# GpSimd takes the adding of squares and every second low half in the gate tiles of a streaming encoder step

## The reference, cut to what matters

```python
xn = rmsnorm(h, norm_mix_g)                  # rsqrt(mean(x*x) + eps), 2048 features
proj = xn @ w_in                             # 2048 x 3584, all in fp32
a = proj[..., :2 * D_CONV]                   # value and gate, 1024 columns each
glu = a[..., :D_CONV] * jax.nn.sigmoid(a[..., D_CONV:])
y = depthwise_conv(glu, 31 taps) + dw_b      # per channel
y = silu(layernorm(y, ln_g, ln_b))
```

## Time and profile before

| | |
|---|---|
| median of 3 runs | 2055.32 us (2044.23, 2055.32, 2055.69) |
| the profiled execution | 2047.77 us, its span 2046.0 us |
| busy in the span | PE 1981.8, DVE 1530.7, ACT 858.1, POOL 718.3 us |
| granted clock of PE, mean | 0.988 |
| slots 1 to 3 of the gate tiles | 32.3 to 51.2 us |
| slots 4 to 15 | 51.2 to 127 us |
| value, key and query | 127 to 220 us |

### The profile page before, as it was taken

One profiled execution on the slowest core, in us unless ns is written; L12 is line 12 of the kernel. 1 busy time (PEld: TensorE's weight loads), 2 busy tenths in 40 slices (PEclk: granted clock), 3 DMA queues, 4 the chain that ended last, 5 costly groups with the idle time before them and its releaser, 6 DMA issues. The chain is left out here.

```text
span 2046.0 us, 29568 instructions
## 1 busy us (share of the span) xinstructions
PE 1981.8 (97%) x11192; PEld 1765.1 (86%) x11192; DVE 1530.7 (75%) x2436; ACT 858.1 (42%) x857; POOL 718.3 (35%) x504
## 2 busy tenths in 40 slices
PE   7999998999899999999999999999999999999997
PEld 6987776998799999999999889988888888888886
DVE  5988745456678788989988987567677777778875
ACT  4340136334334554455454435433434343334343
POOL 2010110220726677587787875011001011114300
PEclk9999998999899999999999999999999999999999
DMA  5464393443344787788888787779998989998983
GB/s 207 164 193 141 116 400 137 153 168 123 127 137 156 247 275 268 272 281 286 274 272 298 265 306 283 294 274 348 340 343 328 343 326 349 364 360 345 372 314 136
DMA packets 101226, 531.27 MB, mean 260 GB/s; under 512 B 19376, under 2 KB 21568, under 8 KB 45792
## 3 DMA queue, kind: packets, MB, share of 16 engines
q1 hardware_dynamic: 71552, 408.93, 55.8%
q0 software_dynamic: 24304, 106.45, 14.4%
q10 hardware_dynamic: 5296, 14.98, 1.9%
HBM read 491.34 MB, written 38.14 MB: 259 GB/s over the span
## 5 line engine op out<-in xcount | busy, mean ns | idle before, releaser
L889 DVE TENSOR_TENSOR wl<-raw,wh 128x2048 fp32r<-128x2048 f32 x310 | 712.4, 2299 | 287.1 <-ACT wh L519 275.5
L519 ACT ACTIVATE wh<-raw 128x2048 fp32r<-128x2048 f32 x310 | 593.3, 1915 | 572.5 <-DMA raw<-in_v 408.4
L1537 PE MATMUL acc<-xhl,wh 128*128 128x448 f32 x2048 | 648.9, 377 | 12.2 <-DVE wl L889 12.2
L1538 PE MATMUL acc<-xhl,wl 128*128 128x224 f32 x2048 | 542.8, 265 | 0.0
L1537 PEld LDWEIGHTS acc<-xhl,wh 128*128 128x128 f32 x2048 | 386.7, 189 | 44.7 <-DVE wl L889 14.6
L1538 PEld LDWEIGHTS acc<-xhl,wl 128*128 128x128 f32 x2048 | 393.2, 192 | 0.0
L2025 POOL DMA_INDIRECT G<-gsum,cell x224 | 348.2, 1554 | 99.7 <-issue 74.8
L1514 PE MATMUL acc<-xhl,wh 128*128 128x288 f32 x768 | 231.7, 302 | 14.8 <-DVE wl L925 14.2
L1515 PE MATMUL acc<-xhl,wh 128*128 128x288 f32 x768 | 228.4, 297 | 0.0
L1516 PE MATMUL acc<-xhl,wl 128*128 128x288 f32 x768 | 227.9, 297 | 0.0
L1514 PEld LDWEIGHTS acc<-xhl,wh 128*128 128x128 f32 x768 | 146.5, 191 | 18.2 <-DVE wl L925 14.2
(11 more groups left out here) (306 smaller groups left out, 2638.8 us busy)
## 6 DMA issues: line engine op xcount, KB each, us to landing
raw<-in_u SPq DMA_DIRECT2D x128, 1024.0 KB
raw<-in_v SPq DMA_DIRECT2D x128, 1024.0 KB
raw<-in_w_mix SPq DMA_DIRECT2D x28, 1024.0 KB
G<-zero SPq DMA_DIRECT2D x16, 1024.0 KB, 13.8
raw<-in_w_out SPq DMA_DIRECT2D x16, 1024.0 KB
raw<-in_w_pq SPq DMA_DIRECT2D x16, 1024.0 KB
gin<-G SPq DMA_DIRECT2D x32, 512.0 KB
h<-hbg ACTq DMA_DIRECT2D x32, 448.0 KB
```

Source lines behind the costliest of these rows:

```text
L519: act.activation(wh[:, n % 4], raw[:, n % 4], ACT.Copy).then_inc(hi_done, 1)
L889: dve.tensor_tensor(wl[:, n % 4], raw[:, n % 4], wh[:, n % 4].bitcast(F32), ALU.subtract).then_inc(lo_done, 1)
L1537: pe.matmul(acc[:, s, 0:2 * NU], wh[:, s, j, :], xu[:, j, 0:2 * NU], start=(j == 0), stop=False)
L1538: ins = pe.matmul(acc[:, s, 0:NU], wl[:, s, j, :], xuh[:, j, :], start=False, stop=(j == DT - 1))
```

## The change

POOL squares two row tiles at a time as before, but adds the results up itself into `sqacc` (in the memory of `gsb`, which is not used yet), without waiting for PE. PE sums `sqacc` by two matmuls, placed between slots 2 and 3. ACT makes the high half of slot 3 before it waits for the sums, DVE the low half of slot 3 before the norm.

In the gate tiles DVE makes only the low halves of even slots from slot 4 on; those of slots 5, 7, 9, 11, 13 and 15 are made by POOL, each behind its multiply of a gate, and counted in the new `odd_lo`. DVE's `lo_done` goes on by two for each even slot.

```diff
@@ ScalarE, glu_iteration @@
-                    if not (last and s >= 4 - AHEAD):
+                    if not (last and s >= 4 - AHEAD) and not (first and s == 1):
                         hi_next(GLU0, i, s)
...
                     if first and s == 0:
+                        hi_next(GLU0, 0, 1)
                         act.wait_ge(eps_ready, 1)
-                        norm_root(0, mis[:, 2], sq_used, 8)
+                        norm_root(0, mis[:, 2], sq_used, 1)
@@ VectorE, glu_iteration @@
-                    if not (last and s >= 4 - AHEAD):
-                        lo_next(GLU0, i, s)
                     if first and s == 0:
+                        lo_next(GLU0, 0, 0)
+                        lo_next(GLU0, 0, 1)
                         norm_recip(0, mis[:, 2])
+                    elif s % 2 == 0 and not (last and s >= 4 - AHEAD):
+                        lo_next(GLU0, i, s, count=2)
@@ TensorE @@
-                pe.wait_ge(lo_done, g + 1)
+                if odd:
+                    pe.wait_ge(odd_lo, 2 * (i - 1) + s // 2 + 1)
+                else:
+                    pe.wait_ge(lo_done, g + 1)
...
             slot(GLU0, 0, 0, xh, xl, before=lambda j: pe.wait_ge(split_lo, j + 1))
-            pe.wait_ge(const_in, 16)
-            squares(0, 2, N)
             for s in range(1, 4):
+                if s == 3:
+                    pe.wait_ge(const_in, 16)
+                    pe.wait_ge(sq_done, 8)
+                    for j in range(2):
+                        ins = pe.matmul(mis[:, 2, 0:N], ones, sqacc[:, j, :], start=(j == 0), stop=(j == 1))
+                    ins.then_inc(sq_used, 1)
                 slot(GLU0, 0, s, xh, xl)
             with pe.Fori(1, 4) as i:
                 for s in range(4):
-                    slot(GLU0, i, s, xh, xl)
+                    slot(GLU0, i, s, xh, xl, odd=s % 2 == 1)
@@ GpSimd @@
-                if n >= 2:
-                    pool.wait_ge(sq_used, n - 1)
                 src = hT[:, 2 * n:2 * n + 2, :]
-                pool.tensor_tensor(sqb[:, n % 2], src, src, ALU.mult).then_inc(sq_done, 1)
+                if n == 0:
+                    pool.tensor_tensor(sqacc[:], src, src, ALU.mult).then_inc(sq_done, 1)
+                    continue
+                pool.wait_ge(sq_done, n)
+                own.done(pool.tensor_tensor(sqb[:, 0], src, src, ALU.mult))
+                own.wait(0)
+                pool.tensor_tensor(sqacc[:], sqacc[:], sqb[:, 0], ALU.add).then_inc(sq_done, 1)
             pool.dma_start(glu[:, :, S0:S0 + HIST], dr["cconv"]).then_inc(hist_in, 16)
...
+            for n in range(8):
+                pool.wait_ge(sig_done, n + 1)
+                pool.wait_ge(acc_free, GLU0 + 4 + 2 * n)
+                if n == 0:
+                    pool.wait_ge(rstd_done, 1)
+                pool.tensor_tensor(gsb[:, 2, :], gsb[:, 1, :], rstd[:, 1, :], ALU.mult).then_inc(sgr_done, 1)
+                if 1 <= n < 7:
+                    g = 2 * n + 3
+                    pool.wait_ge(hi_done, GLU0 + g + 1)
+                    pool.tensor_tensor(wl[:, g % 4], raw[:, g % 4], wh[:, g % 4].bitcast(F32), ALU.subtract).then_inc(odd_lo, 1)
```

More of the change, by code:

```diff
@@ L326, in build @@
         hi_done, lo_done, slot_used = sem("hi_done"), sem("lo_done"), sem("slot_used")
+        odd_lo = sem("odd_lo")
         acc_free = sem("acc_free")
@@ L563, in _ @@
             act.wait_ge(lo_done, VKQ0)
+            act.wait_ge(odd_lo, 6)
             act.sem_inc(hi_done, OUT0 - VKQ0)
@@ L884, in _, with lo_next @@
             own = Own(dve, dve_own)
-            def lo_next(base, i, s, stride=4):
+            def lo_next(base, i, s, stride=4, count=1):
                 n = s + AHEAD
                 dve.wait_ge(hi_done, slot_no(base, i, s, stride) + AHEAD + 1)
-                dve.tensor_tensor(wl[:, n % 4], raw[:, n % 4], wh[:, n % 4].bitcast(F32), ALU.subtract).then_inc(lo_done, 1)
+                dve.tensor_tensor(wl[:, n % 4], raw[:, n % 4], wh[:, n % 4].bitcast(F32), ALU.subtract).then_inc(lo_done, count)
             def slot_ready(base, i, s, stride=4):
@@ L1519, in product, with slot @@
                 return ins
-            def slot(base, i, s, mh, ml, cols=N, before=None, stride=4, freed=None):
+            def slot(base, i, s, mh, ml, cols=N, before=None, stride=4, freed=None, odd=False):
                 g = slot_no(base, i, s, stride)
-                pe.wait_ge(lo_done, g + 1)
+                if odd:
+                    pe.wait_ge(odd_lo, 2 * (i - 1) + s // 2 + 1)
+                else:
+                    pe.wait_ge(lo_done, g + 1)
                 pe.wait_ge(acc_free, g + 1)
@@ L1539, in u_slot @@
                 ins.then_inc(slot_used, 1)
[L1541 to L1544, removed]
+            slot(GLU0, 0, 0, xh, xl, before=lambda j: pe.wait_ge(split_lo, j + 1))
+            for s in range(1, 4):
+                if s == 3:
+                    pe.wait_ge(const_in, 16)
+                    pe.wait_ge(sq_done, 8)
                     for j in range(2):
-                        ins = pe.matmul(mis[:, bank, 0:cols], ones, sqb[:, n % 2, j, 0:cols], start=(c == 0 and j == 0), stop=(c == 7 and j == 1))
+                        ins = pe.matmul(mis[:, 2, 0:N], ones, sqacc[:, j, :], start=(j == 0), stop=(j == 1))
                     ins.then_inc(sq_used, 1)
-            slot(GLU0, 0, 0, xh, xl, before=lambda j: pe.wait_ge(split_lo, j + 1))
-            pe.wait_ge(const_in, 16)
-            squares(0, 2, N)
-            for s in range(1, 4):
                 slot(GLU0, 0, s, xh, xl)
@@ L1895, in _ @@
                     pool.wait_ge(x_in[n // 2], 16)
-                if n >= 2:
-                    pool.wait_ge(sq_used, n - 1)
                 src = hT[:, 2 * n:2 * n + 2, :]
-                pool.tensor_tensor(sqb[:, n % 2], src, src, ALU.mult).then_inc(sq_done, 1)
-            pool.dma_start(glu[:, :, S0:S0 + HIST], dr["cconv"]).then_inc(hist_in, 16)
[L1901 to L1908, removed]
+                if n == 0:
[5 more added lines that the diff above has]
+                pool.tensor_tensor(sqacc[:], sqacc[:], sqb[:, 0], ALU.add).then_inc(sq_done, 1)
+            pool.dma_start(glu[:, :, S0:S0 + HIST], dr["cconv"]).then_inc(hist_in, 16)
+            for n in range(8):
[8 more added lines that the diff above has]
+                    pool.tensor_tensor(wl[:, g % 4], raw[:, g % 4], wh[:, g % 4].bitcast(F32), ALU.subtract).then_inc(odd_lo, 1)
             pool.wait_ge(acc_free, VKQ0 + 4)
```

## The result

| | before | changed |
|---|---|---|
| median of 7 runs each | 2053.05 us (2044.23 to 2055.69) | 2068.78 us (2064.05 to 2073.6) |
| the profiled execution | 2047.77 us, span 2046.0 | 2068.78 us, span 2066.9 |
| granted clock of PE, mean | 0.988 | 0.984 |

The ratio of the times is 1.0075, with a 95% interval of 1.0059 to 1.0091: slower by 15.7 us, under the 1% taken as the bound. The two profiled executions differ by 20.9 us in span, so either figure is to be taken with some microseconds of scatter. The page still shows PE as what bounds the kernel, as in the earlier trace rows; DVE works 24 us more and POOL 46 us more.

A forecast was written before the change was run, and what follows sets the result against it. PE, busy 97% of the span, was taken as the bound. Slot 1 gained only 0.5 us, slot 4 came +5.8, and POOL's low halves brought slot 15 to +15.6; 2051.5 + 15.6 gave 2067 us, range 2050 to 2080.

The forecast's parts named there:

- the squares take 9.75 us of it: PE's stretch from 22.55 to 32.30 before slot 1: 9.75 us removed, about 1.05 us added for two matmuls.
- GpSimd and VectorE exclude each other: Operations with two SBUF inputs on POOL and DVE wait for each other; one of d us takes about d - 0.2.
- In turns: POOL and DVE alternate whole operations; beside the squares two low parts take about 2.75 us instead of 0.88.
- The clock in slot 1: Whether slot 1 starts at 1.2 GHz after slot 0 half busy: 0 to +2 us, taken as 0.
- The norm later, slot 4 idle: Sums seen by ACT at 45.8; slot 4 starts at 57.0 against 51.2, PE idling 5.3 us: +5.8.
- The low half on POOL: Gate tiles: a low half of 2048 elements takes POOL 4.6 us, bounds 3.6 and 6.9.
- The loop: Gate of slot 4 to that of slot 12, bound by DVE: 62.15 us instead of 53.35.
- both shifted alike: Past the projections PE waits for the rope on DVE as before, both equally late.
- (a): Rival: DVE gets several splits in per POOL gap, slowing the loop but not the head; +6.6, 2054.4 us profiled; chance 0.15.
- (b): Rival: no exclusion that matters in head or loop; -1.5 us, 2046.3 us; chance 0.05.
- (c): Rival: clearly slower, POOL's low half costs 6.9 us in the loop; +29, 2077 us profiled; chance 0.22.
- (d): The case as forecast for the whole kernel: +10 to +20 us; chance 0.57.

The follow-up runs named there:

- The last kernel: Against the kernel before: ACT squares x in four operations, DVE adds them up, one matmul between slots 1 and 2, all low halves on DVE; 2046.38 us, 0.9964.

## Why the prediction was right, and which term was off

1. **PE is what counts, and the squares take 9.75 us of it: right.** The last kernel shows that most of it can be saved: 8.0 us at the mark.
2. **GpSimd and VectorE exclude each other: right, and this decided the result.** The low parts were forecast to end at 29 to 29.5 and ended at 30.38; slot 1 was forecast at 31.8 and began at 32.64. The 0.8 is not from the low parts themselves (1.29 us each, forecast 1.38): their row began 0.9 later, at 14.90 and not 14.03, because the low half of slot 0 waited too, 3.05 instead of 2.29. The prediction let it slow POOL, but not POOL it. Delaying the squares brought the 5.24 us back, and the product of two tiles beside DVE stopped it for 4.3 us without any semaphore between them. "In turns" was too strict: a waiting POOL operation can see two of DVE's go by (5.26 us for one of 1.15).
3. **The clock in slot 1: the mis-sized term.** The prediction named 0 to +2 us and took 0, because a stretch half busy had kept the full clock. Here PE was busy 5.0 of 8 us, in pieces, and the clock fell: 24 matmuls at 0.24 us instead of about 0.13, some 2.7 us. The kernel with filling matmuls took away just this and stood 2.76 us earlier at the mark. That one stretch of 2 us at full clock was too little to take 0 from.
4. **The norm later, slot 4 idle: right.** ACT saw the sums at 49.38, forecast 45.8; the difference of 3.6 is 0.8 from slot 1 and 2.8 from its clock. From there to slot 4 were 11.3 us (forecast 11.2), with 5.06 us of idleness (5.3). PE ran slot 4 at 1.2 GHz until 65.90, and the slot took 8.84 us and not 6.35, 2.5 more (about 2 forecast). What hides it is not what the prediction named: PE came to slot 5 at 69.54, POOL's low half had been done at 67.96, and there was no wait. It is DVE, the bound of the loop, on which PE waits again from slot 11 on; of the "1 to 2 us before most later gate slots" only the last five have one.
5. **The low half on POOL: right.** 4.59 to 4.96 us, forecast 4.6; of the rival's 6.9 nothing is seen. The Trainium skill (GPSIMD Engine Reference, 3.1) has 4497 ns for a two-input add of this size; the shortest subtract here, 4592, is 2% longer.
6. **The loop: right.** Gate of slot 4 at 70.03 (forecast 66.4, the 3.6 of point 4), then 61.78 us to that of slot 12 (62.15), then slot 15 at 139.68 (136.3): 3.4 later than forecast, the 3.6, less 0.4 in the loop, and 0.2 behind it.
7. **The whole.** The sum has a slip: 127.9 - 0.4 - 6.35 is 121.15 and not 120.7, so its own terms give +15.1 at slot 15, not +15.6. Slot 15 began at 121.36 before, the delay there is +18.3, and what is missing is the 3.4 of point 6, less 0.2 for where slot 15 stood before. All of it, within 0.15 us, is still there at the first matmul behind the gate tiles (127.70 before, 146.15 now) and at the mark: the projections gave nothing back, and PE's 3.4 us of waits for the rope are the same in both, so "both shifted alike" was right. The medians differ by 15.7. That this is the +15.6 of the prediction is luck: a clock taken at 0 that cost 2.8, a slip of 0.45 the other way, and a part behind the mark which the change does not touch and which scatters by more than that. What makes it scatter stays open. In the 23 runs of the kernel before on one chip it goes with the mean granted clock (2057.2 to 2063.1 us in the four at 0.985 or less, 2045.0 to 2051.1 in the five at 0.990 or more), in the 16 on another, at 0.986 to 0.990, it hardly does. Open is also why in the kernel with six products of two tiles the median rose by 26.4 us with 19.3 at the mark.
8. **The rivals.** (a) fell with 15.48 us for the low parts; (b) with the loop's 61.8 us; (c) with 4.84 us for POOL's low half. (d) held, at +18.45 within its +10 to +20, with the cold clock in slot 1 that it had counted as a help to (c).

## What to carry to other kernels

In these runs work given to GpSimd was not taken off VectorE when VectorE was busy at that time with two operands in SBUF: look up in a trace whether the two run beside each other, and count the duration on GpSimd against what it relieves (here 4.4 against 2.2 us). Before counting a gain on a saturated engine, follow what the new order does to the stretch before it: the gaps in TensorE's slot 0 cost twice here, 4.6 us as waits and 2.8 in the clock of the matmuls that followed. An engine that is idle there and holds up neither, as ScalarE here, is the first to ask.

## What was not expected of the hardware

- On GpSimd the product of 128x2048 with a constant took longer (5.40 to 5.62 us) than that of two tiles (4.64 to 4.88), and the copy 1.89 to 2.16. The Trainium skill (GPSIMD Engine Reference, 4.1) calls one-input work roughly line-rate; the copy can pass for that (VectorE takes 2.29 us for a two-input operation of this size), the product with a constant cannot.
- The product with a constant stopped VectorE for 3.3 of its 5.6 us only, and let it run beside the rest; the product of two tiles stopped it for 4.3 of 4.9. A memset of the same tile, 1.8 us, did not stop it at all.
- The granted clock fell in a stretch in which TensorE still worked 5.0 of 8 us, with gaps of up to 0.93 us between its matmuls; with 5.69 of 8 us, in the kernel with filling matmuls and gaps of up to 0.54 us, it stayed at 1.00.
